# A two-block transformer kernel on one core: the second block's first attention with its values stationary, and the work around it dealt out anew

## The reference, cut to what matters

```python
m = jax.nn.silu(cond) @ w + b                    # adaln: shift, scale, gate, for own tokens and for context
q = rms_norm_2(q, q_norm_g); k = rms_norm_2(k, k_norm_g)   # a norm and 64 gains for each head
q, k = axial_rope(q), axial_rope(k)              # own tokens; the context is not turned
s = einsum('bqkgd,bskd->bkgqs', qg, k) * dh**-0.5          # 8 query heads, 2 key/value heads of 64
p = softmax(s)                                   # own queries see 512 keys, context queries 256
o = einsum('bkgqs,bskd->bqkgd', p, v)
y = concat(conv, o) * silu(z);  x = x + gate * (y @ ab_w_out)
```

## Time and profile before

| | us |
|---|---|
| median of three runs (1127.70 to 1129.18) | 1129.09 |
| the profiled execution | 1128.63 |
| its span | 1126.8 |
| PE busy in it | 1090.4 |
| DVE busy | 751.0 |
| ACT busy | 549.0 |
| POOL busy | 43.6 |

### The profile page before, as it was taken

How to read it: one execution, slowest core, us unless ns; L and a number is a source line. 1 busy time by engine, 2 the same in 40 slices (tenths; PEclk the granted TensorE clock), 3 DMA queues, 4 the chain that set the end, 5 groups by cost and what they waited for, 6 DMA issues and landing times. The chain is left out here.

```text
span 1126.8 us, 17866 instructions
## 1 busy us (share of the span) xinstructions
PE 1090.4 (97%) x7000; PEld 943.2 (84%) x7000; DVE 751.0 (67%) x1456; ACT 549.0 (49%) x985; POOL 43.6 (4%) x55
## 2 busy tenths in 40 slices
PE   8999999999999999999999999999999999999996
PEld 7877879899887877879999988798867888989865
DVE  5774766555555665776887888789765745834475
ACT  5642845444444443855444454535445733623273
POOL 1000001000000000000000000100300000000000
PEclk9999999999999999999999999999999999999998
DMA  9667055555565567047666546843356022864000
GB/s 339 244 217 297 6 164 169 190 190 189 178 203 168 186 203 288 2 150 176 186 206 202 187 159 206 276 150 113 113 192 210 2 88 65 209 159 142 28 18 39
DMA packets 55046, 183.34 MB, mean 163 GB/s; under 512 B 20788, under 2 KB 33460, under 8 KB 35508
## 3 DMA queue, kind: packets, MB, share of 16 engines
q1 hardware_dynamic: 54964, 182.22, 49.5%
HBM read 179.31 MB, written 2.90 MB: 162 GB/s over the span
## 5 line engine op out<-in xcount | busy, mean ns | idle before, releaser
L236 DVE TENSOR_TENSOR w_lo<-ring,w_hi 128x1024 fp32r<-128x1024 f32 x260 | 317.1, 1223 | 203.5 <-ACT w_hi L230 198.7
L230 ACT CAST w_hi<-ring 128x1024 fp32r<-128x1024 f32 x260 | 271.5, 1052 | 323.5 <-PE banks L292 319.5
L292 PE MATMUL banks<-shared_hi,w_hi 128*128 128x256 f32 (+1 forms) x448 | 134.2, 299 | 1.5 <-DVE w_lo L236 1.5
L292 PE MATMUL banks<-shared_lo,w_hi 128*128 128x256 f32 (+1 forms) x448 | 133.7, 298 | 0.0
L292 PE MATMUL banks<-shared_hi,w_lo 128*128 128x256 f32 (+1 forms) x448 | 133.6, 298 | 0.0
L292 PE MATMUL banks<-w_hi,u_hi 128*128 128x512 f32 x256 | 100.0, 390 | 0.0
L292 PE MATMUL banks<-w_lo,u_hi 128*128 128x512 f32 x256 | 99.8, 390 | 0.0
L292 PE MATMUL banks<-w_hi,u_lo 128*128 128x512 f32 x256 | 99.7, 390 | 0.0
L292 PEld LDWEIGHTS banks<-shared_hi,w_hi 128*128 128x128 f32 x448 | 85.7, 191 | 4.2 <-issue 1.7
L292 PEld LDWEIGHTS banks<-shared_hi,w_lo 128*128 128x128 f32 x448 | 85.7, 191 | 2.6
L292 PEld LDWEIGHTS banks<-shared_lo,w_hi 128*128 128x128 f32 x448 | 85.7, 191 | 2.4
(11 more groups left out here) (404 smaller groups left out, 2246.4 us busy)
## 6 DMA issues: line engine op xcount, KB each, us to landing
ring<-in_w_up SPq DMA_DIRECT2D x32, 1024.0 KB, 5.1
ring<-in_w_down SPq DMA_DIRECT2D x32, 1024.0 KB, 5.1
ring<-in_w_in SPq DMA_DIRECT2D x23, 1024.0 KB, 5.2
ring<-in_ab_ada SPq DMA_DIRECT2D x12, 1024.0 KB, 5.2
ring<-in_cd_ada SPq DMA_DIRECT2D x12, 1024.0 KB, 5.0
ring<-in_cd_in SPq DMA_DIRECT2D x12, 1024.0 KB, 7.5
ring<-in_w_out SPq DMA_DIRECT2D x8, 1024.0 KB, 6.6
ring<-in_ab_in SPq DMA_DIRECT2D x16, 512.0 KB, 5.1
```

Of the source, the lines that this page charges most:

```text
L230: nc.scalar.copy(w_hi[:, n % PARTS, :], part_source(key, q)).then_inc(hi_ready, 1)
L236: nc.vector.tensor_tensor(w_lo[:, n % PARTS, :], part_source(key, q), w_hi[:, n % PARTS, :].bitcast(F32), ALU.subtract).then_inc(part_read ...
L292: mm = nc.tensor.matmul(dst, a, b, start=first_one and i == 0, stop=last_one and i == 2, skip_group_check=shares_bank)
```

## The change

- `SECOND_SLABS`, `ADA_AT`: the heads' stage multiplies two slabs of conditions instead of three; the last slab (`cd_late`) comes after `ab_out` in the ring and is multiplied at the end of `out_project`.
- `project_and_convolve`: POOL multiplies the gains of the head norms into the rotation's tables (eight instructions of 64 columns); two small DMAs bring the gains as columns; the last addition of squares is gone, and PE adds the two halves in the variance's matmuls.
- `prepare_axial_heads`: no gains on DVE; the rotation's four products become eight with the new tables; the variance's matmuls stand here; no `keep_busy`.
- `transpose_groups`: the context's half of each group is copied with the gain as its scale; the turn of the conditions moves to the next half's norm (`turn_gates`).
- `attend_by_feature` replaces `attend`: six buffers of transposed probabilities, four of probabilities; the scaling of each 128x512 unit is on GpSimd for two units of three (`on_pool(u)` is `u % 3 != 2`) and on VectorE for the third; values are stationary; results lie by feature in two banks, so the 16 transposes before the output product fall away. At its end the first two parts of `ab_out` are split.
- `out_project` and `project_features`: the context's half of the second addition to x, one of the two splits of `cd_in` ahead and the turn of two slabs' conditions move to the next stage; the DMAs of the gates move to its end.

```diff
-          "cd_first": (1, 0, 2), "cd_heads": (1, 2, 3), "cd_turn": (1, 5, 1)}
+          "cd_first": (1, 0, 2), "cd_heads": (1, 2, 2), "cd_turn": (1, 4, 1), "cd_late": (1, 5, 1)}
-SECOND_SLABS = [("cd_first", 2), ("ab_in", 6), ("cd_heads", 3), ("cd_turn", 1), ("ab_out", 2), ("cd_in", 6), ("cd_out", 2)]
+SECOND_SLABS = [("cd_first", 2), ("ab_in", 6), ("cd_heads", 2), ("cd_turn", 1), ("ab_out", 2), ("cd_late", 1),
+                ("cd_in", 6), ("cd_out", 2)]
...
+                    def turn(i):
+                        wait_scaled(pe, i)
+                        if i >= 2:
+                            pe.wait_ge(turned_copied, i - 1)
+                        for c in range(0, BANK, P):
+                            mm = nc.tensor.transpose(banks[:, T + i % 2, c:c + P], probs[i % HELD][:, c:c + P], ident[:])
+                        mm.then_inc(probs_turned, 1)
...
+                        pair = (i, i + 2)
+                        for r in range(len(units[i]["rows"])):
+                            n_chunks = len(units[i]["rows"][r][4])
+                            for c in range(n_chunks):
+                                for u in pair:
+                                    _, _, c0, _, vs, out = units[u]["rows"][r]
+                                    mm = nc.tensor.matmul(out, vs[c], probsT[u % TURNED][:, c0 + c * P:c0 + (c + 1) * P],
+                                                          start=c == 0, stop=c == n_chunks - 1)
...
+                    for w in range(n_units):
+                        if on_pool(w):
+                            pool.wait_ge(inverted, w + 1)
+                            for r, (_, _, c0, n, _, _) in enumerate(units[w]["rows"]):
+                                here = probs[w % HELD][:, c0:c0 + n]
+                                last = nc.gpsimd.tensor_tensor(
+                                    here, here, inverse[:, w % SUMS, r:r + 1].broadcast_to([P, n]), ALU.mult)
+                            last.then_inc(scaled_pool, 1)
...
+                    for i in range(n_units + SCALE):
+                        w = i - SCALE
+                        if w >= 0:
+                            invert(w)
+                        if i < n_units:
+                            find_max(i)
+                        if w >= 0 and not on_pool(w):
+                            scale(w)
+                        advance(more, 1)
...
                     if attended is not None:
                         pe.wait_ge(gated, len(tiles))
-                        keep_busy(0, 12)
+                        pe.wait_ge(half_used, first["cd_late"])
+                        adapt_products(pe, "cd_late", 0, 0)
+                        keep_busy(1, 6)
...
+                    split_lo(dve, key, 1)
+                    right = slice(BANK, 2 * BANK)
+                    for t in (2, 3):
+                        nc.vector.tensor_tensor(x[:, t, right], mixed[:, t, right], x[:, t, right],
+                                                ALU.add).then_inc(ctx_added, 1)
                     norm["vector"](dve)
...
-            SLABS, TURNED = 3, 3
+            SLABS, TURNED = 2, 3
                 def _(pe):
+                    for t in range(4):
+                        tok = slice(BANK + t * P, BANK + (t + 1) * P)
+                        accumulate(banks[:, VARIANCE, 4 * t:4 * t + 4],
+                                   [(mixed[:, c, tok], minus_half[:, 0:4]) for c in range(2)])
                     for j in range(SLABS):
                         adapt_products(pe, "cd_heads", j, j)
...
-                    keep_busy(7, 12)
```

More of the change, by code:

```diff
@@ L496, in on_tensor @@
                     turn(b)
-                if shifts is not None:
+                if behind is not None:
+                    behind()
+                elif shifts is not None:
                     keep_busy(0, 8)
@@ L609, in _ @@
                     mm.then_inc(spread_ready, 1)
[L610 to L612 removed]
+                    keep_busy(VARIANCE, 5)
                 @block.gpsimd
@@ L979, in _ @@
                         split_own(split_hi, act, key, q)
-                        if attended is not None and q == 0:
-                            high(0)
                         if attended is not None and q == 1:
-                            for g in range(1, 4):
+                            for g in range(4):
                                 high(g)
@@ L2557, in second_block @@
+                                      for i in range(5)], ("cd_turn", 5, turn_row), scatter_bias)
                     units = []
-                    for i in range(B_HEADS // 2):
-                        lanes = [slice(kv * HD, (kv + 1) * HD) for kv in range(B_KV)]
-                        heads = [i + kv * B_HEADS // 2 for kv in range(B_KV)]
+                    for g in range(B_KV):
+                        pairs = [(i, kv) for i in (2 * g, 2 * g + 1) for kv in range(B_KV)]
                         vs = [[proj[:, t, AB_V0 + kv * HD:AB_V0 + (kv + 1) * HD] for t in range(4)]
@@ L3005, in _ @@
                         turn_conditions(cd_rows[:, j, :], banks[:, TURNED, 16 * j:16 * (j + 1)]).then_inc(turned, 1)
-                    keep_busy(7, 12)
-                def apply_gains(tiles):
-                    T = tiles.stop - tiles.start
-                    for h0, h1, gain in ((0, B_HEADS, gains[:, 0:HD]), (B_HEADS, H, gains[:, HD:2 * HD])):
-                        here = qk[:, tiles, h0:h1, :]
-                        last = nc.vector.tensor_tensor(
-                            here, here, gain.unsqueeze(1).unsqueeze(1).broadcast_to([P, T, h1 - h0, HD]), ALU.mult)
-                    return last
                 @block.scalar
```

295 lines of the change are left out of this document (212 added, 83 removed).

## The result

The changed kernel takes 1120.90 us (median of 4 runs, 1117.68 to 1122.31) against 1128.76 before (4 runs, 1127.70 to 1129.18): ratio 0.9931, 95% interval 0.9919 to 0.9944. The forecast was 1118.3 us, in a range of 1112.5 to 1126. The profiled execution took 1120.63 us, its span is 1118.8.

What follows compares the result with a forecast made beforehand. TensorE's queue was taken to bound the kernel, the change touching it between 830 and 960 us. Terms -0.6 - 9.1 - 0.5 + 2.0 - 3.8 + 0.4 + 0.8 = -10.8 us gave 1118.3 us, range 1112.5 to 1126.

Steps and rivals of the forecast that it cites:

- End of the projection: End of the projection: one 128x512 addition on VectorE goes; gain 0.6 us, bounds 0 and 0.7.
- Heads' stage: Heads' stage up to the first transpose: DMA wait and 12 identity matmuls go, 8.1 to 8.2 us instead of 17.25; gain 9.1.
- Transposes: Transposes before the attention: the conditions' turn goes, keep_busy grows from three to five matmuls, copies are split; gain 0.5 us.
- Clock: Transposes before the attention: the clock falls at about 840.5 without the identity matmuls; loss 2.0 us, bounds 0 and 5.3.
- Attention: First scores to first output product: fill 11.0, seven pairs at 3.5, tail 12.4; 47.9 us against 51.7, gain 3.8.
- GpSimd: Scaling in the attention: a 128x512 product takes 1.3 us alone, 2 to 2.5 beside VectorE, which makes GpSimd stand still.
- Output product: End of the output product: the late slab's products and ScalarE's copy come before its half of x; loss 0.4 us.
- next stage: Stage after the output product: a split and two additions precede VectorE's first hidden-state instruction, TensorE waits; loss 0.8 us.
- A: Rival: the clock stays low into the attention, costing 5.3 instead of 2.0 us and some 1 more; 1122.5 us, chance 0.16.
- B: Rival: GpSimd paces the attention at 2.1 us a product, 4.4 a pair; 8 us more, 1126.3 us, chance 0.12.
- C: Rival: VectorE keeps GpSimd out in the attention, 4.1 us a product, 5.5 a pair; slower, 1131.8 us, chance 0.09.
- D: Rival: no early start, as halves for cd_turn come 4 us late and attention's gain is eaten; 1126 us, chance 0.06.

## Why the prediction held, and which terms were off

The mechanism held: less work and no DMA wait in TensorE's queue ahead of the attention, and a shorter attention. Two terms of the sum were mis-sized, the clock and the attention's tail, and one price was right by luck.

- *Bound and place*: right. Everything came out of TensorE's queue between 830 and 960 us.
- *End of the projection*, -0.6: measured 2.62 to 2.02, -0.60. Of the point ahead of it: it stands at 828.04 to 828.25 in the changed kernel's variants without an early fall of the clock and at 829.59 to 829.95 in those with one. Both the kernel before and the changed kernel have one, so the +0.45 is something else, and stays open.
- *Heads' stage*, -9.1 with 8.15 us left of 17.25: mechanism right, no DMA wait, VectorE and ScalarE hidden. With the fall 9.58 are left; without one, in the kernel with the splits drawn forward, 7.88.
- *Transposes*, -0.5: -0.45.
- *Clock*, +2.0: mis-sized, and the first step that failed. I put one fall at 840.5, because the work ahead of it was the same. But the falls are not bound to a place: one came at 834 here, at 832.6, 836.7 or not at all in variants, at 884 and 887 in two, and even the first 450 us, where TensorE has the same instructions in all kernels, have one at 96, one at 435 or none. And one came at 950, in a stage that I never asked about, where the change puts 16 narrow turns in the place of 16 identity records and 0.75 us of wait behind them. In this profile the two falls cost 3.4 us, 1.4 more than my term.
- *Attention*, -3.8, measured -2.28: fill 10.59 (forecast 11.0), seven pairs 24.65 (24.5), tail 14.17 (12.4). The tail was mis-sized by 1.8 us, the second step that failed: its term of 7.6 us for TensorE's list had no waits in it. The list it names (scores, six transposes, three value groups) took from 883.34 to 893.04, 9.7 us, with waits of 0.84, 0.49 and 0.55 for GpSimd's product and ScalarE's copies. What follows, a copy, the splits and the stage entry, took 4.4 us from the copy's start, as counted. That the splits needn't stand there is shown by drawing them forward, for 1.6 us.
- *GpSimd*: my 1.3 us alone was 1.04. The Trainium skill's price (GPSIMD Engine Reference, Performance versus the Vector engine) had given an estimate of 1.1, and the trace agrees with it. The 2 to 2.5 us in the attention did not come, and a sign that I had named for being wrong did: VectorE's own instructions were lengthened by GpSimd, by 5.0 us in all, which I had counted at nothing. I had read the 4.13 us of the earlier trace rows as GpSimd's weakness. But the 128x512 products start behind an inversion, while VectorE reads PSUM, so GpSimd gets hold of the path first, and VectorE is the one that waits. Where GpSimd starts second it waits, as its 128x256 products of 0.92 to 1.51 us show; the 4.13 us fit that, but no run tests them. The Trainium skill (SBUF — State Buffer, SBUF: two separate sides) states just this, that whoever starts first has the pair for its whole instruction, and here the later one ends 0.47 to 0.54 us behind the earlier one; I should have drawn it from there. The 3.5 us a pair was luck: I had GpSimd and TensorE equally loaded in every pair, where four pairs run at TensorE's own 3.26 and the mean is lifted by single waits, 0.92 of them for the gatings that I had not counted.
- *Output product* +0.4 and *next stage* +0.8: +0.38 and +0.89.
- *Rivals*: A is refuted: the clock is 1.00 in the first pairs, and five profiles show it returning under transposes. B needed a product of 2.1 us and C one above 3.5; the 128x512 products took 1.04. D did not come: products of `cd_turn` wait for nothing.

The sum missed by 2.8 us: 1.4 for the clock, 1.5 for the attention, the rest cancels. Both lay on the same side; the range held them.

## What to carry to other kernels

When work is cut from a stage, the last thing that ends it changes: write down each engine's own list to its last instruction, above all what prepares the next stage, and let it start where that engine idles; and count the waits between the engines, for a list without them came out 2 us short here. Before giving another engine a share, ask who holds the shared path first; here the engine that was relieved paid back five eighths of what it was spared (5.0 of 8.1 us). Where the clock falls at times, judge a change by time and mean granted clock over several runs, beside the kernel before on the same chip, never by one trace's fall.

## What the hardware showed

- A GpSimd product of 128x512 with a broadcast operand took 1.04 us, 128x256 0.61 where nothing held it up. A two-input SBUF instruction of VectorE that started inside one ended some 0.54 us behind it; a 128x256 product that started inside VectorE's instruction ended 0.47 or 0.48 us behind that, and so took 0.92 to 1.51. VectorE's maximum of 0.67, whose input lies in PSUM, wasn't lengthened.
- Apart from the run's end, the low stretches lasted 3.4 us or twice that in all 13 profiles that record them, and whether and where one lies differs between kernels with the same instructions up to there. The clock's share of a run is 3 to 11 us, of which the run's end, without cost, is 2.0 to 3.2 in the profiles; it explains four fifths of the spread between runs of a kernel.
- Identity matmuls did not always prevent a fall: of eight records in the heads' stage the last ones ran at 0.50. The clock came back under transposes alone in five profiles.
